# Cache copies moved out of the input projection, and a new order at both ends of the down phase

## The chip, the cores and the metric

One core of one Trainium2 chip runs the whole program. Times are device microseconds of one execution. The five engines are TensorE (PE), VectorE (DVE), ScalarE (ACT), GpSimd (POOL) and SyncE (SP). SP, ACT and POOL start DMA transfers.

## What is computed

One hybrid decoder layer, once on a new prompt of 1024 tokens and once on 8 x 8 new tokens that follow 8192 cached ones. Everything is float32.

```python
def decoder_layer(x, pos, ret_state, k_buf, v_buf, ...):
    z = rmsnorm(x, g_pre_mix) @ w_in                   # 1024 -> 3584
    ... rotary phases on rq, rk; chunkwise retention; group norm; silu gate -> ro
    ... softmax attention, windows (128, 1), (512, 4), (2048, 16), shared bias -> ao
    k_new, v_new = k_all[:, T:], v_all[:, T:]          # the cache, moved on by 8 rows
    x = x + rmsnorm(concat([ro, ao]) @ w_out, g_post_mix)
    gate, up = split(rmsnorm(x, g_pre_ffn) @ w_gu)     # 1024 -> 2 x 2816
    f = (silu(gate) * up) @ w_down                     # 2816 -> 1024
    return x + rmsnorm(f, g_post_ffn), S_new, k_new, v_new
```

The sample's two cache outputs are the inputs moved on by 8 rows: 2040 of 2048 rows of each of 8 sequences are a plain copy from HBM to HBM, 67 MB in all.

## The kernel before

Six stages follow one another: input projection, retention, prompt attention, sample attention, output projection, and the feed-forward part, which has a gate and up phase and a down phase. Each float32 operand is split into a high and a low part (ACT makes the high one, DVE the low one), and PE multiplies high by high, high by low and low by high.

**The cache copies.** `copy_windows` (L127) issues two transfers on POOL's queue, one for the keys and one for the values, of 34 rows of each of 8 sequences: one of 60 shares. Nothing waits for them until the end of the program. Before, 24 shares are issued in the input projection (one after every second tile of z, L343), 32 in the gate and up phase (`PACED`, one or two after the second block of each half group) and 4 in the down phase, after steps 5, 16, 27 and 38.

**Input projection.** For seven groups of 512 columns and nine tiles of rows PE makes z in a PSUM bank, ACT or POOL puts it into one of four buffers `z_out`, and SP stores it to z_scratch. A buffer is free again when its store has landed. Weights of 1 MB per half come on SP's queue.

**Prompt attention.** It has 32 units (four pairs of heads by eight tiles of rows); a pair's later tiles have more keys. For each unit POOL makes two scaled identities `diag` from the softmax denominators, which PE uses two units later. SP loads q, k and v of a pair (512 KB each, in pieces of 512 bytes) while the pair before it runs, and the keys of the second sequence for sample attention after the second pair's. Sample attention loads 5.2 MB of keys and values for each sequence.

**Output projection.** For each tile of rows t, POOL does rstd, the residual sum xm, rstd again and `low` of tile t - 1.

**Gate and up.** Group 0 is apart; groups 1 to 10 (`LAST`) have two half groups of eight blocks, each block a product in the manner of Strassen's seven products. ACT and DVE work six blocks ahead of PE (`LEAD`) into a ring of eight slots (`slot_hi`, `slot_lo`). The last operations of a group give f in six parts, counted by `f_ready`; they read the banks chain_a, chain_b, rest_ps[0] and rest_ps[1]. f and its sums and the differences of w_down go to HBM (`store_f`, `store_f_sums`, `store_t`), since the down phase begins only when all of f is made.

**Down phase.** Seven products P1, P2, P6, P7, P5, P4, P3 of eleven groups each. The first six make 66 steps; a step is four pairs of 128 rows, each three matmuls of 512 columns. Step s needs two operands of 256 KB from HBM, which SP loads into `raw_step[s % 4]` once DVE has made the lows of step s - 4. The bank of pair i in P1 is (x_ps[0], x_ps[1], rest_ps[0], chain_a)[i]; P2 takes chain_b, rest_ps[1] and the two banks of the sample. PE waits in `pair_free` at the first step of each product. The last product P3 has its own 22 blocks, loaded by `load_last(g)` into two buffers `raw_last`, split by `split_last(m)` and `low_last(m)` between the steps' blocks, and used by PE after step 65. `load_last(g)` waits for `low_last(2g - 3)`. SP, like every engine, works through its queue in order.

## Time and profile before

| | us |
|---|---|
| median of 3 runs | 1629.06 |
| lowest and highest | 1626.73 and 1633.83 |
| profiled execution | 1639.63 |
| its span, first to last instruction | 1637.8 |
| PE busy in the span | 1508.8 |
| mean granted clock of PE | 0.972 |

The span is what the trace covers, and its starts are counted from the first instruction. The profiled execution took 10.6 us more than the median. The stages begin at about 0 (input projection), 380 (retention), 463 (prompt attention), 621 (sample attention), 732 (output projection), 850 (gate and up) and 1360 (down). In a timeline row, brackets give the idle time before the instruction and what ended it. The page counts a matmul of 512 columns as 0.39 us, but the next starts 0.23 us after it, as they overlap.

### The profile page before, as it was taken

What the parts mean: (1) busy time and instruction counts of PE and PEld (TensorE: products, weight loads), DVE (VectorE), ACT (ScalarE), POOL (GpSimd) and SP (SyncE); (2) the same over time, 40 slices, a digit from 0 to 9 for tenths busy, and PEclk for the clock granted to TensorE, in tenths of its full rate; (3) what the DMA queues carried; (4) which work ended last, traced back from release to release, by engine and by line L of the source; (5) the groups of instructions that cost most, each with busy time, mean ns of one, the idle gap of its engine ahead of it and who ended that gap; (6) DMA issues with size and microseconds to landing.
All of it is one profiled execution on the core that took longest, in us unless ns stands there. A gap on an engine that the chain in (4) does not pass through costs nothing.

```text
span 1637.8 us, 23157 instructions
## 1 busy us (share of the span) xinstructions
PE 1508.8 (92%) x8974; PEld 1292.8 (79%) x8974; DVE 817.4 (50%) x1380; ACT 555.7 (34%) x1046; POOL 326.3 (20%) x366
## 2 busy tenths in 40 slices
PE   7999999798988888989998899999999997999667
PEld 6788877587845556767888899999999996888546
DVE  2333111103866654543559666666676665554435
ACT  4401112112144443442433333333333432544332
POOL 3265421002532223002554000000000010000001
PEclk9999999899999999999999999999999998999789
DMA  5369899846573108973334679978878787876445
GB/s 204 124 164 234 200 202 216 219 125 220 177 245 120 52 14 332 418 285 107 123 116 161 198 189 177 231 218 237 215 182 240 210 214 232 264 221 201 135 160 180
DMA packets 138253, 317.76 MB, mean 194 GB/s; under 512 B 23884, under 2 KB 65116, under 8 KB 132997
## 3 DMA queue, kind: packets, MB, share of 16 engines
q1 hardware_dynamic: 129352, 229.26, 42.5%
q0 software_dynamic: 6976, 71.32, 21.4%
q10 hardware_dynamic: 1824, 15.83, 2.3%
q8 instruction: 65, 1.06, 0.3%
q14 instruction: 36, 0.29, 0.1%
HBM read 254.45 MB, written 137.92 MB: 240 GB/s over the span
## 4 chain that ended last, share of the span: by engine, by line
PE 36%; DVE 6%; DMA 5%; issue 3%; POOL 3%; ACT 1%; SPq 1%; POOLq 0%; ACTq 0%; DVEq 0%
PE y_ps L2676 25%; PE y_ps L2757 4%; DMA raw_step<-wt_scratch 3%; PE x_ps L2757 2%; DVE slot_lo L2419 2%; DMA raw_step<-w_down 1%; DMA raw<-w_gu 1%; POOL xm L1710 1%; POOL h_lo L1722 1%; PE y_ps L2666 1%; PE y_ps L1841 1%; DVE y L1806 1%; PE m_ps L2757 1%; PE d_ps L2757 1%; PE m_ps L2687 1%
## 5 line engine op out<-in xcount | busy, mean ns | idle before, releaser
L518 PE MATMUL z_ps<-w_hi,h_hi 128*128 128x512 f32 x488 | 191.9, 393 | 17.8 <-ACT z_out L392 11.4
L518 PE MATMUL z_ps<-w_lo,h_hi 128*128 128x512 f32 x488 | 190.9, 391 | 0.0
L2676 PE MATMUL y_ps<-h_hi,slot_hi 128*128 128x320 f32 (+1 forms) x560 | 180.4, 322 | 5.5 <-DVE f L2430 5.5
L2676 PE MATMUL y_ps<-h_hi,slot_lo 128*128 128x320 f32 (+1 forms) x560 | 180.3, 322 | 0.0
L2676 PE MATMUL y_ps<-h_lo,slot_hi 128*128 128x320 f32 (+1 forms) x560 | 180.0, 321 | 0.0
L518 PE MATMUL z_ps<-w_hi,h_lo 128*128 128x512 f32 x432 | 169.0, 391 | 0.0
L131 POOL DMA_DIRECT2D ks_sample<-cache_k_win x60 | 34.0, 567 | 609.9 <-PE y_ps L2676 418.9
L2419 DVE TENSOR_TENSOR slot_lo<-raw_step,slot_hi 128x512 fp32r<-128x512 f32 x132 | 85.4, 687 | 128.0 <-ACT slot_hi L2248 127.9
L518 PEld LDWEIGHTS z_ps<-w_hi,h_hi 128*128 128x128 f32 x488 | 92.3, 189 | 39.4 <-ACT z_out L392 11.9
L2248 ACT CAST slot_hi<-raw_step 128x512 fp32r<-128x512 f32 x132 | 75.4, 619 | 138.1 <-DMA raw_step<-wt_scratch 64.6
L2676 PEld LDWEIGHTS y_ps<-h_hi,slot_hi 128*128 128x128 f32 x560 | 105.7, 189 | 5.7 <-issue 5.7
L2676 PE MATMUL y_ps<-s_hi,slot_hi 128*128 128x384 f32 x320 | 107.6, 336 | 0.0
L2676 PE MATMUL y_ps<-s_hi,slot_lo 128*128 128x384 f32 x320 | 107.6, 336 | 0.0
L2676 PE MATMUL y_ps<-s_lo,slot_hi 128*128 128x384 f32 x320 | 107.5, 336 | 0.0
L518 PEld LDWEIGHTS z_ps<-w_lo,h_hi 128*128 128x128 f32 x488 | 92.2, 189 | 18.9
L2676 PEld LDWEIGHTS y_ps<-h_lo,slot_hi 128*128 128x128 f32 x560 | 105.6, 189 | 0.0
L430 DVE TENSOR_TENSOR w_lo<-w_raw,w_hi 128x2048 fp32r<-128x2048 f32 x14 | 34.2, 2450 | 143.0 <-ACT w_hi L365 143.0
L2676 PEld LDWEIGHTS y_ps<-h_hi,slot_lo 128*128 128x128 f32 x560 | 105.5, 188 | 0.0
L518 PEld LDWEIGHTS z_ps<-w_hi,h_lo 128*128 128x128 f32 x432 | 81.6, 189 | 17.1
L2419 DVE TENSOR_TENSOR slot_lo<-raw,slot_hi 128x512 fp32r<-128x512 f32 x104 | 79.8, 786 | 30.2 <-ACT slot_hi L2248 28.8
L2757 PE MATMUL y_ps<-slot_hi,slot_hi 128*128 128x512 f32 x132 | 55.6, 422 | 15.2 <-DVE f L2454 8.7
L2290 ACT COPY held<-y_ps 128x384 f32<-128x384 f32 x60 | 28.7, 479 | 120.3 <-PE y_ps L2676 120.3
(359 smaller groups left out, 3245.2 us busy)
## 6 DMA issues: line engine op xcount, KB each, us to landing
ks_sample<-cache_k_win POOLq DMA_DIRECT2D x60, 544.0 KB, 9.8
vs_sample<-cache_v_win POOLq DMA_DIRECT2D x60, 544.0 KB, 12.2
raw<-w_gu SPq DMA_DIRECT2D x20, 1024.0 KB, 12.6
raw_step<-f_scratch SPq DMA_DIRECT2D x66, 256.0 KB, 3.8
K<-cache_k_win SPq DMA_DIRECT2D x8, 2048.0 KB
w_raw<-w_in SPq DMA_DIRECT2D x14, 1024.0 KB
z_scratch<-z_out SPq DMA_DIRECT2D x56, 256.0 KB, 5.4
raw_d<-w_down SPq DMA_DIRECT2D x11, 1024.0 KB, 9.3
```

The costliest lines, as they stand in the source:

```text
L131: eng.dma_start(flat(new)[:, bass.ds(row * WID, n * WID)], flat(old)[:, bass.ds(row * WID + DEC_T * WID, n * WID)]).then_inc(kept, 16)
L430: dve.tensor_tensor(w_lo[cut], w_raw[:, q], w_hi[cut].bitcast(F32), ALU.subtract).then_inc(w_lo_ready, 1)
L518: mm = pe.matmul(z_ps[t % 3][:, :], x[:, k, t * 128:t * 128 + 128], w[:, par, k, :], start=(k, n) == first, stop=(k, n) == last)
L1710: pool.tensor_tensor(self.xm[:, t % 2, :], self.y[:, :], self.inputs.x_n[:, t % 2, :], ALU.add).then_inc(self.xm_ready, 1)
L1722: pool.tensor_tensor(self.h.lo[at][cut], self.hg[:, q, :, 0:n], self.h.hi[at][cut].bitcast(F32), ALU.subtract).then_inc(self.lo_ready, 1)
L1806: dve.scalar_tensor_tensor(self.y[0:n, :], src[0:n, :], self.stat[0:n, 2:3], self.g_post[0:n, :], ALU.mult, ALU.mult).then_inc(self.y_read ...
L1841: mm = pe.matmul(self.y_ps[t % 2][:, c:c + 512], x[:, t % 2, k, :], w, start=(k, n) == (0, 0), stop=(k, n) == (KT - 1, len(terms) - 1))
L2248: act.copy(in_slot(slot_hi, n), source(n)).then_inc(hi_ready, 1)
L2290: act.copy(held[:, k, :], chain_a[:, 0:384]).then_inc(held_ready, 1)
L2419: dve.tensor_tensor(in_slot(slot_lo, n), source(n), in_slot(slot_hi, n).bitcast(F32), ALU.subtract).then_inc(lo_ready, 1)
L2676: mm = pe.matmul(bank[:, 0:cols], w, v[:, k, :], start=fresh and (k, m) == (0, 0), stop=(k, m) == (HK - 1, 2), skip_group_check=True)
L2757: mm = pe.matmul(bank, x[:, own], w[:, :], start=fresh and m == 0, stop=ends and m == 2, skip_group_check=True)
```

## The change

The shares of the cache copies are issued elsewhere: none in the input projection, 20 in prompt attention (after `diag` of units 6 to 25), 4 in the output projection (tiles 3 to 6), 30 in the first nine groups of the gate and up phase, and 6 in the down phase (after steps 7, 18, 29, 40, 41 and 52). At the start of the down phase the pairs on rest_ps[0] and chain_a wait for 62 and 64 of `f_ready` in place of 66, and the wait for all 66 stands at P2, which uses the other two banks. SP asks for the operands of step 4 before it stores f and w_down's differences of the last group, and DVE makes the sums of the last f after step 1's blocks. `load_last(g)` comes four steps later in SP's order (after the load of step 48 + 2g), its last two after the loop; `split_last` and `low_last` begin two steps later, with the last two blocks at the end. Handing `kept` through is left out below.

```diff
@@ -132,7 +132,7 @@
                       flat(old)[:, bass.ds(row * WID + DEC_T * WID, n * WID)]).then_inc(kept, 16)
 
 
-SHARE, COPIED_FIRST = (L - DEC_T) // 60, 24
+SHARE = (L - DEC_T) // 60
 
 
 def tile_rows(t):
@@ -336,20 +336,9 @@
                                            ALU.subtract).then_inc(lo_ready, 1)
                     rstd(t)
                 pool.wait_ge(ret.tab_landed, ret.TABS)
-                def copies(k, t):
-
-                    n = at(k, t) - TT
-                    if n % 2 and n < 2 * COPIED_FIRST:
-                        copy_windows(pool, A, kept, n // 2 * SHARE, SHARE)
-
                 for k in (*ROTATED, GATED):
                     for t in range(TT):
                         finish(k, t)
-                        copies(k, t)
-                for k in range(GATED + 1, GROUPS):
-                    for t in range(TT):
-                        pool.wait_ge(z_evac, at(k, t) + 1)
-                        copies(k, t)
 
             @block.scalar
             def _(act):
@@ -1060,6 +1049,8 @@
                     for r in range(2):
                         pool.tensor_scalar(diag[:, g % 2, r], ident[:, :], share[:, g, r:r + 1], None,
                                            ALU.mult).then_inc(diag_ready, 1)
+                    if 6 <= g < 26:
+                        copy_windows(pool, A, kept, (g - 6) * SHARE, SHARE)
 
             @block.scalar
             def _(act):
@@ -1712,6 +1703,8 @@
             pool.tensor_tensor(self.stat[:, 5:6], self.stat[:, 4:5], self.mhalf[:, :], ALU.pow).then_inc(self.xm_rstd, 1)
             if t >= 1:
                 self.low(pool, t - 1)
+            if 3 <= t < 7:
+                copy_windows(pool, self.A, self.kept, (t + 17) * SHARE, SHARE)
 
     def low(self, pool, t):
 
@@ -1969,7 +1962,7 @@
     LAST, RING, LEAD = GROUPS - 1, Count.RING, 6
     LATE_PAIRS = 2
     STEPS = GROUPS * P3
-    PACED = [(24 + 8 * n // 5, 24 + 8 * (n + 1) // 5) for n in range(Count.CHAINS)]
+    PACED = [(24 + 5 * n // 3, 24 + 5 * (n + 1) // 3) for n in range(Count.CHAINS - 2)]
     EARLY_TILES, LATE_TILES = (3, 4, 5, 7), (0, 1, 2, 6)
     FINAL = (PT, 3, 4, 0, 5, 1, 7, 2, 6)
     w_gu = A["w_gu"][0].rearrange("(k p) n -> p k n", p=128)
@@ -2164,12 +2157,14 @@
                     else:
                         load_step(2)
                         load_step(3)
-                    store_t(g)
+                    if g < LAST:
+                        store_t(g)
+                load_step(4)
+                store_t(LAST)
                 store_f(LAST)
-                load_step(4)
                 load_step(5)
+                load_step(6)
                 store_f_sums(LAST)
-                load_step(6)
                 load_step(7)
                 sp.wait_ge(f_stored, 48 * GROUPS)
                 sp.wait_ge(f_sum_ready, 4 * GROUPS)
@@ -2179,8 +2174,10 @@
                 load_x(1)
                 for s in range(8, STEPS):
                     load_step(s)
-                    if s >= GROUPS * P5 and (s - GROUPS * P5) % 2 == 0:
-                        load_last((s - GROUPS * P5) // 2)
+                    if s >= GROUPS * P5 + 4 and s % 2 == 0:
+                        load_last((s - GROUPS * P5 - 4) // 2)
+                load_last(LAST - 1)
+                load_last(LAST)
                 for i, t in enumerate(FINAL):
                     sp.wait_ge(y_ready, i + 1)
                     to = (A["y_prompt"][0, t * 128:t * 128 + 128, :] if t < PT
@@ -2222,15 +2219,15 @@
                                    z[SEQ:NTOK, cols].rearrange("(b t) c -> b t c", b=DEC_B)).then_inc(kept, 16)
                 pool.wait_ge(s3_hi_ready, 1)
                 pool.tensor_tensor(s_lo[2][:, :, :], s_sum[2][:, :, :], s_hi[2][:, :, :].bitcast(F32), ALU.subtract).then_inc(s3_ready, 1)
-                for g in range(1, GROUPS):
+                for g in range(1, LAST):
                     for hh in range(2):
                         pool.wait_ge(done, made(g, hh, 1))
                         copies(*PACED[2 * g - 2 + hh])
                 pool.wait_ge(half_set, 2)
                 root(0)
-                for p in range(4):
-                    pool.wait_ge(done, stepped(GROUPS * p + 5))
-                    copies(56 + p, 57 + p)
+                for p in range(6):
+                    pool.wait_ge(done, stepped(GROUPS * p + 7 if p < 4 else GROUPS * p - 3))
+                    copies(54 + p, 55 + p)
                 for i in range(1, TT):
                     root(i)
                 pool.wait_ge(kept, 16 * (4 + 2 * 60))
@@ -2396,8 +2393,11 @@
                             act.copy(y[PT][0:NS, 512 * c:512 * c + 512], sample_ps[c][NS:128, :]).then_inc(sample_low, 1)
                     split_ahead(Count.step(s) + LEAD)
                     split_ahead(Count.step(s) + 1 + LEAD)
-                    if s >= GROUPS * P5:
-                        split_last(s - GROUPS * P5)
+                    if s >= GROUPS * P5 + 2:
+                        split_last(s - GROUPS * P5 - 2)
+                    if s == STEPS - 1:
+                        split_last(2 * GROUPS - 2)
+                        split_last(2 * GROUPS - 1)
                     if s == 8:
                         square(0)
                     if s == GROUPS * P1 + LAST:
@@ -2613,8 +2613,9 @@
                             times(g, 4, rest_ps[1], 1, 2)
                             add_up(g, 2, 10, 5, 1, 0)
                     sample_low_part(g, 1)
-                sums_of_f(LAST)
                 for s in range(STEPS):
+                    if s == 2:
+                        sums_of_f(LAST)
                     if s == Count.SUMMED_AT:
                         for m in range(4):
                             low_ahead(down(LAST, m) + LEAD)
@@ -2624,8 +2625,11 @@
                             dve.tensor_tensor(y[PT][0:NS, cols], sample_ps[c][0:NS, :], y[PT][0:NS, cols], ALU.add).then_inc(folded, 1)
                     low_ahead(Count.step(s) + LEAD)
                     low_ahead(Count.step(s) + 1 + LEAD)
-                    if s >= GROUPS * P5:
-                        low_last(s - GROUPS * P5)
+                    if s >= GROUPS * P5 + 2:
+                        low_last(s - GROUPS * P5 - 2)
+                    if s == STEPS - 1:
+                        low_last(2 * GROUPS - 2)
+                        low_last(2 * GROUPS - 1)
                     if s == 9:
                         dve.wait_ge(half_set, 2)
                         dve.wait_ge(g_landed, 16)
@@ -2736,9 +2740,10 @@
 
                 def pair_free(p, i):
                     if p == P1:
-                        pe.wait_ge(f_ready, 6 * GROUPS)
+                        pe.wait_ge(f_ready, 6 * LAST + (2 if i == 2 else 4))
                     elif p == P2:
                         pe.wait_ge(c_ready, 3 * Count.CHAINS)
+                        pe.wait_ge(f_ready, 6 * GROUPS)
                         pe.wait_ge(folded, 2)
                     elif p == P6:
                         pe.wait_ge(y_copied, i + 1)
```

## Rows read from the trace of the kernel before

**Rows 1.** The page's first part: busy us (share of the span) and instructions of each engine.
```profile
PE 1508.8 (92%) x8974; PEld 1292.8 (79%) x8974; DVE 817.4 (50%) x1380; ACT 555.7 (34%) x1046; POOL 326.3 (20%) x366
```
**Rows 2.** Waits of PE, whole span: total us, times, longest us.
```profile
PE x_ps L2757 <- DVE slot_lo L2419: 20.2, 6, 4.9
...
PE y_ps L2757 <- DVE f L2454: 8.7, 1, 8.7
```
**Rows 3.** Windows, input projection: from:to, length, each engine's busy us (x), PEclk, DMA, GB/s.
```profile
176.00:210.00 34.00, 34.00 (x151) 28.15 (x150) 2.29 (x1) 5.71 (x7) 8.18 (x10) 1.00 0.97 223
200.00:300.00 100.00, 97.87 (x430) 80.38 (x430) 12.72 (x6) 19.27 (x24) 16.33 (x23) 1.00 0.97 203
315.00:325.00 10.00, 8.16 (x25) 6.53 (x26) 2.29 (x1) 3.71 (x4) 1.10 (x2) 0.65 0.72 248
346.00:354.00 8.00, 8.00 (x37) 6.64 (x36) 0.00 (x0) 0.69 (x1) 1.10 (x2) 1.00 0.65 204
```
**Rows 4.** Timeline of PE at 316; then z_out, the store issued at 280.94.
```profile
316.84 0.79 PE L518 MATMUL z_ps<-w_hi,h_hi 128*128 128x512 f32 x1 [11.44 <-ACT z_out L392]
...
DMA to landing us min/median/max: 35.1/35.1/35.1
```
**Rows 5.** Windows in prompt attention and one in sample attention, columns as in rows 3.
```profile
510.00:530.00 20.00, 16.53 (x122) 10.20 (x124) 13.27 (x37) 11.05 (x27) 5.90 (x10) 1.00 0.71 238
545.00:560.00 15.00, 12.70 (x96) 7.93 (x96) 10.01 (x30) 7.89 (x20) 5.51 (x10) 1.00 0.52 140
...
650.00:700.00 50.00, 46.70 (x674) 36.50 (x673) 25.41 (x41) 24.15 (x49) 0.00 (x0) 1.00 1.01 417
```
**Rows 6.** Timelines of POOL, SP and PE in both attentions: start, us, instruction, idle before.
```profile
495.69 1.18 POOL L1061 TENSOR_SCALAR diag<-ident,share 128x128 f32<-128x128 f32 x2 [4.86 <-PE O_ps L1229]
...
584.97 1.18 POOL L1061 TENSOR_SCALAR diag<-ident,share 128x128 f32<-128x128 f32 x2 [1.66 <-DVE share L1155]
...
509.95 0.43 SPq L965 DMA_DIRECT2D q_n<-z_scratch  x1
...
534.39 1.06 PE L1186 MATMUL T_ps<-ident,q_n 128*128 128x128 f32 x8
...
571.02 1.04 PE L1186 MATMUL T_ps<-ident,q_n 128*128 128x128 f32 x8
...
644.17 3.27 PE L1460 MATMUL T_ps<-ident,K 128*128 128x128 f32 x28 [1.55 <-DMA K<-z_scratch]
```
**Rows 7.** Timelines of POOL, ACT and PE, start of the down phase; a window of it.
```profile
1342.88 0.55 POOL L131 DMA_DIRECT2D ks_sample<-cache_k_win  x1 [21.43 <-PE y_ps L2676]
...
1363.91 0.62 ACT L2248 CAST slot_hi<-raw_step 128x512 fp32r<-128x512 f32 x1 [10.48 <-DMA raw_step<-w_down]
...
1370.55 0.80 PE L2757 MATMUL y_ps<-slot_hi,slot_hi 128*128 128x512 f32 x1 [8.69 <-DVE f L2454]
...
1370.00:1380.00 10.00, 9.45 (x29) 7.51 (x30) 6.92 (x12) 3.03 (x6) 0.00 (x0) 0.66 0.86 293
```
**Rows 8.** Down phase: a window, then timelines of PE and ACT.
```profile
1400.00:1480.00 80.00, 79.80 (x350) 65.13 (x349) 42.22 (x66) 36.92 (x67) 3.88 (x7) 1.00 0.75 235
...
1481.57 0.39 PE L2757 MATMUL x_ps<-slot_hi,slot_hi 128*128 128x512 f32 x1
...
1597.79 0.63 PE L2757 MATMUL y_ps<-last_hi,last_hi 128*128 128x512 f32 x1
...
1463.21 0.62 ACT L2248 CAST slot_hi<-raw_step 128x512 fp32r<-128x512 f32 x1 [2.69 <-DMA raw_step<-wt_scratch]
...
1516.85 0.62 ACT L2248 CAST slot_hi<-raw_step 128x512 fp32r<-128x512 f32 x1 [7.16 <-DMA raw_step<-wt_scratch]
```
**Rows 9.** The tile m_n, its two loads issued from 756.3 to 757.
```profile
DMA to landing us min/median/max: 5.2/5.3/5.4
```
**Rows 10.** The page's last part: DMA issues, size of each, median us to landing.
```profile
raw<-w_gu SPq DMA_DIRECT2D x20, 1024.0 KB, 12.6
```

More of the change, by code:

```diff
@@ L977, in __call__, with prompt_attention @@
         return self.nc.alloc_sbuf_tensor_at(name, shape, dtype, offset=here)
-def prompt_attention(nc, A, z, mix_t, bias, ident, q_n, k_n, qk_landed, clear, ahead, second_keys, spare, retained, state_s, S_out, sout_ready):
+def prompt_attention(nc, A, z, mix_t, kept, bias, ident, q_n, k_n, qk_landed, clear, ahead, second_keys, spare, retained, state_s, S_out, sout_ready):
     UNITS, LAST = NPAIR * PT, NPAIR * PT - 1
@@ L1633, with __init__ @@
 class OutProjection:
-    def __init__(self, nc, ctx, A, x_mid, h, ident, inputs, w_b):
+    def __init__(self, nc, ctx, A, x_mid, h, ident, kept, inputs, w_b):
         at = lambda n, s, o, d=F32: nc.alloc_sbuf_tensor_at(n, s, d, offset=o)
@@ L1638, in __init__ @@
         sem = lambda n: nc.alloc_semaphore("p5_" + n)
-        self.A, self.x_mid, self.h, self.ident, self.inputs, self.w_b = A, x_mid, h, ident, inputs, w_b
+        self.A, self.x_mid, self.h, self.ident, self.kept, self.inputs, self.w_b = A, x_mid, h, ident, kept, inputs, w_b
         self.m_hi = at("m_hi", [128, 2, KT, 128], Layout.M_SPLIT, F32R)
@@ L1981, in out_and_ffn @@
         ps = lambda n, s: ctx.enter_context(nc.psum_tensor(n, s, F32))
-        out = OutProjection(nc, ctx, A, x_mid, h, ident, inputs, w_b)
+        out = OutProjection(nc, ctx, A, x_mid, h, ident, kept, inputs, w_b)
         sem = lambda n: nc.alloc_semaphore("p6_" + n)
@@ L2857, in load_first_window @@
             sp.dma_start(q_s[:, :], z[SEQ:NTOK, 4 * WID:5 * WID]).then_inc(q_landed, 16)
-        prompt_attention(nc, A, z, mix_t, bias_p, ident, q_n, k_n, qk_landed, clear_padding, load_first_window,
+        prompt_attention(nc, A, z, mix_t, kept, bias_p, ident, q_n, k_n, qk_landed, clear_padding, load_first_window,
                          lambda sp: load_keys(sp, A, z, K, K_landed, 1),
```

## The prediction

> **What bounds the kernel now.** I read the page first, then PE's waits, then windows of the four stretches that the edits touch. PE is busy 92% of the span [rows 1], so only time in which PE stands or runs at the low clock can be won. The longest waits of PE are six in the down phase for slot_lo and one for f at its start [rows 2], and one of 11.4 us late in the input projection [rows 4]. All three lead to DMA. Matmuls of 512 columns come every 0.228 us at full clock (430 in 97.87 us, rows 3; 350 in 79.8 us, rows 8). The profiled execution took 1639.63 us, 10.6 us over the median of 1629.06; I sum against its trace and take the difference from the median.
>
> **Prices.** A cache share is two transfers of 544 KB, 1.11 MB. One alone fills the window 346 to 354 at a DMA share of 0.65 [rows 3], so it takes 5.2 us of all 16 DMA engines; I use 5.4 (queue start included), 205 GB/s. Beside SP's transfers both are slower. In the window 176 to 210 all engines together moved 223 GB/s at a share of 0.97 [rows 3]; three shares are 98 of it, which leaves SP's queue 125, part of it moved while no copy was pending. SP's loads alone run at about 320 GB/s (0.75 of the engines carry 235 in the down phase, rows 8). I use 100 GB/s for SP's queue while copies are pending.
>
> **1. Input projection: 24 shares go.** ACT waited for a free z_out because a store landed 35.1 us after its issue; PE stood 11.44 us [rows 4]. Then the granted clock was low: 25 matmuls took 8.16 us between 315 and 325 [rows 3], 2.5 us over 0.228 each. From 200 to 300 PE stood 2.1 us more. Sum 16.0 us. Without copies SP's queue there has 2 MB of weights, 1 MB of zr and nine stores of 256 KB in 49 us, under 120 GB/s: nothing is late next. Gain 16, bounds 11 and 16.
>
> **2. Prompt attention: 20 shares come, one after each of the units 6 to 25.** In the trace these units' diag operations run from 495.69 to 584.97 [rows 6]: 89 us for 20 x 5.4 = 108 us of DMA. POOL's own 1.1 us for the two issues lies in its idle time before the next diag (1.1 us at the shortest), so PE pays nothing for it; if POOL's queue filled, POOL would hold back diag and PE, but then the copies are done earlier, and the balance below stays.
> The other traffic here is 0.71 x 20 + 0.52 x 15 [rows 5] and some 2 us of stores, 24 us. Together 132 us from 497, to 629. While both run, the window 176 to 210 does 98/205 + 125/320 = 0.87 of the work that the engines could; the 24 us last some 63 us then and lose 8. So the queue is empty at 637. Sample attention begins at 621.3 and runs at 417 GB/s with a DMA share of 1.01 [rows 5], and its keys landed 1.55 us late already [rows 6]: what is left over delays it one for one, 16 us.
> Inside the stage: the q and k rows of the third pair are asked for at 509.95 and used at 534.39, those of the fourth at 546 and used at 571.02 [rows 6]. At 100 GB/s the first 1.57 MB land at 528, in time; the values and second keys hold the queue until 557, and the fourth pair's rows land at 574: 3.5 us late, and some slow clock. I take 5. **Cost 21 us.** Below, if the engines take the copies in beside the rest without loss and finish at 629: 9 us. Above: 50 us, if SP's queue gets 60 GB/s: the third pair's rows come 2 us late and the fourth's 43.
>
> **3. Output projection: 4 shares.** POOL has 2.9 us free after low in each tile. The rows of the next tile landed after 5.2 to 5.4 us [rows 9] and were used at once, so they have no slack; but they are asked for some 8 us after low, when the copy (7 us) is through. Cost 1 us, bounds 0 and 8.
>
> **4. Gate and up.** 30 shares over 18 half groups in place of 32 over 20: the same two or one per half group, and PE never stood there. Nothing.
>
> **5. The start of the down phase.** Two shares were issued from 1342.88, and a load of w_down for step 2, issued at 1343.31, held ACT for 10.48 us until 1363.91; DVE's last f came behind it, and PE, which wants all six f before its third pair, stood 8.69 us [rows 7]. Then 29 matmuls took 9.45 us at a granted clock of 0.66, 2.8 us over 0.228 each [rows 7]. The change removes both: the last group has no copies, and the third and fourth pairs wait for the second and fourth f only, which free their banks. Next late would be the lows of steps 0 to 2 or the loads of steps 5 and 7, asked for behind stores of f and of its sums; load 4 goes out 20 us earlier, and sums_of_f (four operations of 0.7 us) moves to step 2, where DVE has two steps in hand. Gain 11.5, bounds 7 and 12.
>
> **6. The last product's blocks.** PE begins step 39 at 1481.57 and the last product at 1597.79 [rows 8]: 116.2 us for 27 steps of 12 x 0.228 = 2.74, 74.0 us. So 42 us are lost. The reason is in SP's order. load_last(g) at s = 44 + 2g waits for low_last(2g - 3), which DVE does at its step 41 + 2g; the load of step 45 + 2g queues behind it and is wanted at DVE's next step. So every two steps hold one full trip from issue to landing, and ACT stands 7.16 us in it [rows 8]. After the change the wait at s = 48 + 2g ends at DVE's step 43 + 2g, and the load of step 49 + 2g is wanted at 46 + 2g: two steps lie between. A trip of 6 us, 0.63 us of ACT and 2.5 of DVE make 9 us for three steps, and with one step of DVE (1.9 us) 11 for four; PE needs 10.9. So PE may just set the pace. But the traffic is then 1.57 MB in two steps, 288 GB/s, and two shares (57 and 58) are issued at steps 40 and 41 and one at 52. One share alone made ACT wait 2.69 us for a load and cost PE 0.6 [rows 8]: it ate the 6 us in hand. Two hold SP's queue to 100 GB/s for 16 to 20 us, while 4.9 MB are wanted: 9 us; the one at 52 costs 4; slow clock 2 to 3. Residue 16 of 42. **Gain 26 us**, bounds 14 (every trip lengthened) and 38.
> The last product's blocks 9 and 10 come after the loop; its first pass needs block 10 only after 10 x 3 x 0.228 = 6.8 us, which covers that load. The tail of 1637.8 - 1597.8 = 40 us stays.
>
> **Sum.** -16 + 21 + 1 - 11.5 - 26 = -31.5 us, or 1598 us.
>
> **The rivals.**
> (a) The copies fit: prompt and sample attention pay 5 us, and the down phase 5. For it: the engines are idle half of 495 to 621. Against: 89 us for 108. -16 + 5 - 11.5 - 37 = -59.5, 1570 us.
> (b) The down phase stays bound by loads: a trip of 9 us (a share's neighbours took 8 to 9.7) makes 13.4 us for four steps, 3.35 each, over 18 steps 11 us more. 1609 us.
> (c) The wait at the start stays, on something else late in DVE's chain; PE then waits some 9 us as now. 1609 us.
> (d) Slower. The DMA engines take turns between the copies' queue and SP's by pieces, not by bytes. In 176 to 210 SP's queue moved about 1660 pieces of 2 KB in 34 us, 49 per us. q and k of one pair are 2048 pieces of 512 bytes: 42 us, landing at 552 where 534 is wanted, 18 us late. For the fourth pair the values (21 us), keys and store (11) and q and k (42) come to 626 against 589, 37 late. With the clock 61 us in place of 21, and nothing left for the next stage: 1638 us. It decides once SP's queue moves fewer than some 85 pieces per us beside copies. Against it: the gate and up loads of 1 MB are 1024 pieces of 1 KB, most of them issued within 1 us of one or two shares, and landed after 12.6 us in the median [rows 10]: some 97 per us, twice the pieces at the same bytes.
> The Trainium skill says, in "DMA: Bandwidth & Descriptors", section "Queues, rings and completion order", that each engine goes round the queues by packets of about 9 to 17 descriptors, whatever they hold. By that rule (d) would hold, as 512 byte rows make the smallest packets; the trace of before has no such rows beside copies, so it neither agrees nor disagrees. The same page, "Issuing engines are not separate DMA queues", says transfers from all engines share 16 DMA engines, which rows 3 and 5 bear out.
>
> **How the numbers follow.** Forecast 0.50 (1598, own range 1582 to 1612), (a) 0.14, (b) 0.15, (c) 0.05, (d) 0.11, something not seen 0.05. The range 1572 to 1626 leaves out (d) and most of (a)'s lower half. A measurement of this kernel tells about 0.5%, 8 us, from no change. Faster by more than that: the forecast, (a), (c) and nearly all of (b), 0.81. Within it 0.09, slower 0.10.
>
> **What would show it.** Right: no wait of PE for z_out; PE going on at the third pair of step 0 without a pause; ACT's waits for raw_step under 3 us from step 48 on but for two places behind the shares; the start of sample attention near 625 less 16, with keys 10 us or more late in its first periods. The prediction is wrong if prompt attention has long waits for q_n and k_n (d), if none of its transfers is late (a), or if raw_step still holds ACT in every pair of steps (b).

## The result, and the profile after

The changed kernel takes 1667.47 us in the median of four runs (1664.31 to 1676.02), the kernel before 1627.89 in the median of four beside them. The ratio is 1.026, 95% interval 1.019 to 1.034: slower by about 40 us, where 1598 us and faster was forecast. The profiled execution took 1664.31 us.

The page's first part and its DMA queues (part 3: packets, MB, share of 16 engines) of the changed kernel:

```profile
PE 1492.7 (90%) x8974; PEld 1284.4 (77%) x8974; DVE 816.2 (49%) x1380; ACT 556.6 (33%) x1046; POOL 327.1 (20%) x366
...
q1 hardware_dynamic: 129352, 229.26, 41.0%
q0 software_dynamic: 6976, 71.32, 23.4%
```

PE works 16 us less than in [rows 1] in a span that is 25 us longer. q1 is SP's queue; q0 is POOL's, nearly all of it the copies. Waits of PE in the changed kernel:

```profile
PE T_ps L1177 <- DMA k_n<-z_scratch: 82.9, 2, 42.7
...
PE x_ps L2762 <- DVE slot_lo L2419: 4.6, 2, 4.3
...
PE z_ps L507 <- POOL h_lo L335: 4.3, 3, 1.8
...
PE y_ps L2762 <- DVE slot_lo L2419: 1.0, 1, 1.0
```

The waits of [rows 2] have become small: 4.6 us for slot_lo on the banks x_ps in place of 20.2, and f at the start of the down phase is gone. The wait for z_out of [rows 4] is gone too. In their place stand two waits for k_n, 82.9 us, half of the time in which PE isn't busy (1662.5 - 1492.7 = 169.8). Timelines of the changed kernel show them (PE and SP; in brackets the idle time before):

```profile
442.65 1.09 PE L1177 MATMUL T_ps<-ident,q_n 128*128 128x128 f32 x8 [1.07 <-POOL ones L1043]
...
487.50 0.43 SPq L954 DMA_DIRECT2D q_n<-z_scratch  x1
487.98 6.14 SPq L954 DMA_DIRECT2D k_n<-z_scratch  x1
494.16 51.45 SPq L1018 DMA_DIRECT2D v_n<-z_scratch  x1
...
552.15 1.97 PE L1177 MATMUL T_ps<-ident,q_n 128*128 128x128 f32 x8 [40.19 <-DMA k_n<-z_scratch]
...
567.71 1.06 SPq L954 DMA_DIRECT2D k_n<-z_scratch  x1
...
635.19 1.97 PE L1177 MATMUL T_ps<-ident,q_n 128*128 128x128 f32 x8 [42.67 <-DMA k_n<-z_scratch]
...
687.74 4.99 PE L1451 MATMUL T_ps<-ident,K 128*128 128x128 f32 x44 [0.34 <-PEq L1009]
```

Rows asked for at 487.5 come at 552, and SP stands for 51 us in the very next issue. Prompt attention begins 21 us earlier than before (442.65 against 463.59) and ends 66 us later (687.74 against 621.29): it takes 245.1 us in place of 157.7.

Lengths of the stretches, each from the first matmul of a stage to that of the next (step 39 by counting 468 matmuls; the last stretch to the end of the span):

| | before | after |
|---|---|---|
| start to prompt attention | 463.6 | 442.7 |
| prompt attention | 157.7 | 245.1 |
| sample attention to gate and up | 739.0 | 740.5 |
| down phase, to step 39 | 121.3 | 108.9 |
| step 39 to the last product | 116.2 | 82.2 |
| last product to the end | 40.0 | 43.1 |

-20.9 + 87.4 + 1.5 - 12.3 - 34.0 + 3.1 is the 24.8 us between the two spans. Every part but one won what it should or more; the last stretch, which was to stay, grew by 3.1 us.

### The profile page after: what moved, and what is told of

The parts are those of the page before. It is cut to its first block, busy times and chain, and to the rows that moved or that the text cites. A ratio compares the mean times of both kernels' runs of the same rounds, so it can differ in the third digit from the quotient of the medians.

```text
span 1662.5 us, 23144 instructions
## 1 busy us (share of the span) xinstructions
PE 1492.7 (90%) x8974; PEld 1284.4 (77%) x8974; DVE 816.2 (49%) x1380; ACT 556.6 (33%) x1046; POOL 327.1 (20%) x366
## 4 chain that ended last, share of the span: by engine, by line
PE 36%; DVE 5%; POOL 3%; DMA 3%; issue 3%; ACT 1%; SPq 1%; POOLq 0%; ACTq 0%; DVEq 0%
PE y_ps L2680 26%; PE y_ps L2762 4%; PE x_ps L2762 3%; DMA raw_step<-wt_scratch 2%; DVE slot_lo L2419 2%; POOL xm L1701 1%; DMA raw<-w_gu 1%; POOL h_lo L1715 1%; PE y_ps L2670 1%; PE y_ps L1834 1%; DVE y L1799 1%; PE m_ps L2691 1%; PE d_ps L2691 1%; DVE y L2519 1%; SPq L2108 0%
## 5 line engine op out<-in xcount | busy, mean ns | idle before, releaser
L419 DVE TENSOR_TENSOR w_lo<-w_raw,w_hi 128x2048 fp32r<-128x2048 f32 x14 | 32.0, 2289 | 124.1 <-ACT w_hi L354 124.1
L1177 PE MATMUL T_ps<-ident,q_n 128*128 128x128 f32 x32 | 6.2, 355 | 83.9 <-DMA k_n<-z_scratch 82.9
L1050 POOL TENSOR_SCALAR diag<-ident,share 128x128 f32<-128x128 f32 x64 | 37.9, 599 | 175.0 <-DVE share L1146 133.8
## 6 DMA issues: line engine op xcount, KB each, us to landing
raw_d<-w_down SPq DMA_DIRECT2D x11, 1024.0 KB, 12.3
```

The source lines that it names most:

```text
L419: dve.tensor_tensor(w_lo[cut], w_raw[:, q], w_hi[cut].bitcast(F32), ALU.subtract).then_inc(w_lo_ready, 1)
L1050: pool.tensor_scalar(diag[:, g % 2, r], ident[:, :], share[:, g, r:r + 1], None, ALU.mult).then_inc(diag_ready, 1)
```

## What holds the rows back: the trace of the changed kernel

The windows of the first wait (columns as in rows 3):

```profile
487.50:530.00 42.50, 20.90 (x158) 13.21 (x158) 17.02 (x44) 12.89 (x30) 13.96 (x25) 0.85 1.02 159
530.00:552.00 22.00, 0.00 (x0) 0.00 (x0) 0.00 (x0) 0.00 (x0) 0.00 (x0) 0.50 0.89 154
```

The DMA engines are full, but at 159 GB/s. The packets tell whose they are. DMA queues of the changed kernel from 500 to 515, and then from 545 to 554 (packets, MB, share):

```profile
DMA packets 344, 1.89 MB, mean 126 GB/s; under 512 B 125, under 2 KB 289, under 8 KB 291
...
q0 software_dynamic: 171, 1.78, 94.5%
q1 hardware_dynamic: 171, 0.09, 3.8%
...
q1 hardware_dynamic: 2607, 2.28, 83.0%
q0 software_dynamic: 43, 0.10, 5.5%
```

In the first window one packet of SP's queue (some 520 bytes) goes for one packet of the copies (10.4 KB on the mean): 171 and 171, and 199 and 199 between 580 and 600. SP gets 6 GB/s. The mean of 10.4 KB mixes two sizes: only 53 of the 344 packets hold 8 KB or more, and 51 of them, of 34 KB each, carry the copies' 1.78 MB; their other 120 are under 512 bytes. In the second window the copies are through, and SP's queue moves 2607 packets in 9 us. The landings agree: the share issued at 511.4 landed at 546.6 (keys) and 549.9 (values), q at 549.3 and k at 552.1; in the second case the last values landed at 633.7, q at 632.8 and k at 635.1. **The rows land when the pile of copies is through.**

The trace of the kernel before had shown the same in small. A load of w_gu in pieces of 1 KB was issued at 935.1, with two shares behind it. Its DMA queues from 935 to 940, and then from 940 to 948:

```profile
q1 hardware_dynamic: 1005, 1.02, 62.8%
q0 software_dynamic: 40, 0.56, 38.3%
...
q0 software_dynamic: 95, 1.11, 99.5%
q1 hardware_dynamic: 35, 0.03, 3.1%
```

Nearly the whole load had gone by 940, when the copies' packets filled the engines; the last few dozen packets took until 948.3.

The second cause is the pile itself. The first two shares, issued 6 us apart, landed after 5.9 to 7.0 us. From the fourth on (issued every 3 to 6 us) each landed 8.6 us after the one before, on the mean: nine issued between 474 and 511 were through at 550, where 5.4 us each would have made 523. From the rows of 500 to 515, a 34 KB packet held its engine for an estimated 4.4 us (94.5% of 16 x 15 us, by 51).

## The experiments

### The parts one by one

Theory 1: the copies in prompt attention do it, by turns of packets. Its rivals: the amount of bytes, or the order in SP's own queue. The first four runs have 1631.09 us (seven runs) as their time before.

```diff
-                    if 6 <= g < 26:
-                        copy_windows(pool, A, kept, (g - 6) * SHARE, SHARE)
```

> The changed kernel without the 20 shares of prompt attention; they are left out, so 20 of 60 shares of the two cache outputs are not written. Every theory that puts the loss on these copies expects both waits of PE for q_n and k_n (40.2 and 42.7 us) gone and the low clock beside them too: sample attention starts 82.9 + some 4 us earlier, and the whole takes about 1664 - 87 = 1577 us. If the q and k rows are late for another reason (the order in SP's queue, a wait before their issue), one of the two waits stays and the time is above 1610 us.

Measured: 1582.66 us, ratio 0.970 (0.964 to 0.975). No wait for k_n; q and k land after 4.8 and 6.1 us, and the stage takes 159.4 us. The order in SP's queue is that of the changed kernel, so it is not the cause.

```diff
-                    if 6 <= g < 26:
-                        copy_windows(pool, A, kept, (g - 6) * SHARE, SHARE)
...
-            if 3 <= t < 7:
-                copy_windows(pool, self.A, self.kept, (t + 17) * SHARE, SHARE)
...
+                    if n % 2 and n < 2 * COPIED_FIRST:
+                        copy_windows(pool, A, kept, n // 2 * SHARE, SHARE)
```

> The changed kernel with its 24 shares of prompt attention and output projection back in the input projection, as in the kernel before. Parts 2 and 3 are undone, and so is part 1. What is left is the new start of the down phase and the later asking for the last product's blocks, which the trace of the changed kernel puts at some 42 us from sample attention to the end: about 1628 - 40 = 1588 us. If the down phase's gain came from the shares' new places in gate and up and down alone it would be the same here; if it came from PE having been slow or late earlier in the changed kernel, 1610 us or more.

Measured: 1594.14 us, ratio 0.977 (0.971 to 0.983), 37 us below its own runs of before and 6 above the number given. The wait for z_out is back (12.0 us). From sample attention to the end it takes 976.6 us, the changed kernel 974.8, the kernel before 1016.5: the gain of the down phase has nothing to do with the early shares. Against e1_no_att_copies, which has none there, the 24 shares in the input projection cost 11.5 us.

The kernel before with its 24 early shares in their new places:

```diff
-SHARE, COPIED_FIRST = (L - DEC_T) // 60, 24
+SHARE = (L - DEC_T) // 60
...
+                    if 6 <= g < 26:
+                        copy_windows(pool, A, kept, (g - 6) * SHARE, SHARE)
...
+            if 3 <= t < 7:
+                copy_windows(pool, self.A, self.kept, (t + 17) * SHARE, SHARE)
```

> The kernel before with only its first 24 shares moved: none in the input projection, 20 in prompt attention, 4 in the output projection; gate, up and down are as before. Parts 1, 2 and 3 alone. From the two traces: the input projection wins 21 us, prompt attention loses 87, the output projection about nothing: 1628 + 66 = 1694 us. If the losses in the changed kernel had come from elsewhere, about 1634 us, as predicted for these three parts.

Measured: 1705.64 us, ratio 1.046 (1.040 to 1.051), 12 us above the number given; prompt attention began at 448.9 here, 6 us later than in the changed kernel, and the rest wasn't looked into. Waits for k_n of 81.5 us, the stage 244.0 us, and the waits for slot_lo of before are still there. Together with e1 and e2 this puts the loss on these 20 shares alone.

### Turns by packets

```diff
+def copy_rows(eng, A, kept, row, n):
+    rows = lambda name, at: A[name][0].rearrange("b l h d -> l b (h d)")[at:at + n]
+    for new, old in (("ks_sample", "cache_k_win"), ("vs_sample", "cache_v_win")):
+        eng.dma_start(rows(new, row), rows(old, row + DEC_T)).then_inc(kept, 16)
...
-                        copy_windows(pool, A, kept, (g - 6) * SHARE, SHARE)
+                        copy_rows(pool, A, kept, (g - 6) * SHARE, SHARE)
```

> The changed kernel with the 20 shares of prompt attention asked for in pieces of 2 KB (row by row) in place of pieces of some 10 KB; the bytes are the same. Theory 1, the engines take turns between the queues by pieces: a turn of the copies then carries a fifth of the bytes, SP's 512-byte pieces go some two to five times as fast while both are pending, and the two waits of PE for k_n fall from 83 us together to under 35; about 1610 us, and sample attention finds some copies left over. Theory 2, the engines share by bytes or the sum of all transfers sets the time: the waits stay within 5 us of 83, or grow if small pieces make the copies dearer: 1660 us or more. POOL may take longer to issue a copy; if that holds diag back, PE's waits for diag say so.

Measured: 1693.61 us, ratio 1.038 (1.032 to 1.044). Its longest wait of PE, and its DMA queues from 505 to 518, when copies were pending throughout:

```profile
PE O_ps L1222 <- POOL diag L1057: 97.8, 6, 24.5
```
```profile
DMA packets 4358, 2.56 MB, mean 197 GB/s; under 512 B 2198, under 2 KB 3984, under 8 KB 4350
...
q0 software_dynamic: 2534, 1.52, 56.0%
q1 hardware_dynamic: 1824, 1.05, 32.3%
```

The packets of the copies are now of 600 bytes on the mean. Again two sizes are mixed: 366 packets of 4 KB carry nearly all of the 1.52 MB (twice the 2 KB I had asked for, about an eighth of 34 KB), and the rest are under 512 bytes. SP's queue gets 1.05 MB in 13 us, 81 GB/s in place of 6. Fewer shares were pending here than in the changed kernel's window (under two, where it had four or five), but the copies moved as fast, 117 GB/s against 119. q and k of the third pair land after 16.2 and 24.5 us in place of 61.8 and 64.1, and no wait for k_n is left. So the turn theory holds: the same bytes in small packets let SP through. The time missed theory 1's 1610 by 84 us, by another way of starving: POOL stood for up to 23 us in issuing a copy, and diag behind it. That its queue took no more is the likely reason, not shown. The shares landed 10.9 us apart on the mean.

### The down phase

Both are e2_copies_back with one part undone; the runs before them took 1634.5 us in the median. The first excerpt leaves out that the later loads among the stores, the sums of f and `PACED` (now 30 shares over 20 half groups) go back too.

```diff
-                for g in range(1, LAST):
+                for g in range(1, GROUPS):
...
-                load_step(4)
-                store_t(LAST)
+                store_t(LAST)
                 store_f(LAST)
+                load_step(4)
...
-                        pe.wait_ge(f_ready, 6 * LAST + (2 if i == 2 else 4))
+                        pe.wait_ge(f_ready, 6 * GROUPS)
```

> The kernel of e2_copies_back (both new ends of the down phase, copies of the attention back in the input projection), with the old start of the down phase: copies in the last group too (30 over 20 half groups), the loads of steps 4 to 6 behind the stores, all six f before PE's third pair, the sums of the last f before step 0. The difference to e2_copies_back prices part 5. If the prediction's 11.5 us are right: 1594 + 11.5 = 1605.5 us, with a wait of PE for f near 9 us at the start. If the wait at the start moves elsewhere (rival c): 1596 us. If the start is worth more than predicted, 1609 us or more.

Measured: 1596.27 us, ratio 0.974 (0.970 to 0.978): 2 us from e2_copies_back, less than these runs tell apart, so the old order alone is not worth the 11.5 us. The wait for f is 2.3 us. To step 39 it takes 113.1 us, where e2_copies_back takes 108.9 and the kernel before 121.3. The two differ from before in the copies too: one share in the last group's first half in place of two. That needn't be what made the 8 us: e3_copies_only has the old start with the very copies of before, and takes 115.9 us, with waits of 4.7 us for f and 6.5 us of ACT for the load of [rows 7] (before 8.7 and 10.5, here 2.3 and 4.1). So the old start costs 4 to 12 us over the new one, by the kernel that it stands in, and what part the copies have in it isn't shown.

```diff
-                    if s >= GROUPS * P5 + 4 and s % 2 == 0:
-                        load_last((s - GROUPS * P5 - 4) // 2)
-                load_last(LAST - 1)
-                load_last(LAST)
+                    if s >= GROUPS * P5 and (s - GROUPS * P5) % 2 == 0:
+                        load_last((s - GROUPS * P5) // 2)
...
-                    if s >= GROUPS * P5 + 2:
-                        low_last(s - GROUPS * P5 - 2)
+                    if s >= GROUPS * P5:
+                        low_last(s - GROUPS * P5)
```

> The kernel of e2_copies_back with the last product's blocks asked for as before (load_last two steps after each other from step 44 on, split and made low two steps earlier); shares stay where e2_copies_back has them. The difference prices part 6. From sample attention to the end the changed kernel won some 40.5 us by parts 5 and 6; if the start took 11.5 of them, this one is 29 us slower than e2_copies_back: 1623 us, with six waits of PE for slot_lo of some 20 us together as before. By the predicted 26 us it would be 1620, by the bound of 14 it would be 1608.

Measured: 1635.08 us, ratio 1.000 (0.998 to 1.002): by the two ratios some 38 us slower than e2_copies_back, more than the 29 I had left for this part. Waits of PE, and the last product's first matmuls:

```profile
PE x_ps L2761 <- DVE slot_lo L2421: 19.6, 6, 4.6
...
PE y_ps L2761 <- DVE slot_lo L2421: 11.9, 4, 4.4
```
```profile
L2761 PE MATMUL y_ps<-last_hi,last_hi x22: 387/389/398, 1597.4 to 1611.9; 128*128 128x512 f32 x22
```

From step 39 to the last product the old order takes 124.1 us here, the new one 83.9. In the kernel before it took 116.2, and in e3_copies_only 117.6. The shares of steps 40, 41 and 52 stand in this stretch only in the changed kernel and those made from it; they are what differs, and the old order takes 6.5 to 8 us more with them.

### The same 20 shares elsewhere

From the landings so far I took a share for 6 us, and the pile for SP's transfers only. Both kernels are the changed one with other units:

```diff
-                    if 6 <= g < 26:
-                        copy_windows(pool, A, kept, (g - 6) * SHARE, SHARE)
+                    if g in PLACES:
+                        copy_windows(pool, A, kept, PLACES.index(g) * SHARE, SHARE)
```

> The changed kernel with the same 20 shares in prompt attention after other units: 5 to 7, 12 to 15, 19 to 31 in place of 6 to 25, so that no more than one is pending when SP asks for the q and k rows of a pair, and the last pair, in which SP loads nothing, takes eight. Theory 1 (turns by pieces, so that 512-byte rows starve whenever copies stand beside them): both waits for k_n go, the stage costs no more than the 3 to 8 us by which the last copies reach into sample attention: 1583 + 6 = 1589 us, with both bounds 1583 and 1600. Theory 2 (108 us of copies are too much for this stage wherever they stand): the stage keeps more than half of its loss, 1625 us or more.

> As e7_20_elsewhere, with 16 shares in prompt attention (units 5, 6, 13 to 15, 19 to 22, 24 to 30) and four in the input projection (after tiles 5, 17, 29 and 41 of z). Theory 1: nothing of the 16 is late, sample attention starts on time, and four shares 66 us apart hold no store of z for longer than some 10 us, so the input projection pays nothing: 1583 us, within 4. If even single shares cost the input projection time (the 24 cost 11.5 us, about 0.5 each), 1585 us. If theory 2 holds, 1610 us or more.

Measured: 1649.03 us (ratio 1.007, 1.004 to 1.009) and 1622.67 us (0.992, 0.989 to 0.994). Both miss theory 1 as I had priced it, by 60 and 40 us, and lie where theory 2 put them. Waits of PE in e7_20_elsewhere, a timeline of POOL at the start of sample attention, and three windows with little but copies in them:

```profile
PE T_ps L1451 <- PEq L1009: 41.6, 1, 41.6
PE T_ps L1177 <- DMA k_n<-z_scratch: 25.8, 1, 25.8
```
```profile
671.98 0.52 POOL L1336 MEMSET V_second<- 128x512 f32 x1 [48.84 <-POOLq L1009]
```
```profile
478.00:484.00 6.00, 4.97 (x41) 4.03 (x39) 4.53 (x12) 3.70 (x9) 2.16 (x5) 1.00 0.56 192
603.00:625.00 22.00, 17.86 (x148) 12.22 (x145) 13.00 (x29) 9.53 (x19) 9.68 (x18) 1.00 1.02 123
...
633.00:670.00 37.00, 0.00 (x0) 0.00 (x0) 0.00 (x0) 0.00 (x0) 0.00 (x0) 0.51 0.91 121
```

Three things are read here. First, from 603 to 625 SP moves next to nothing (6 packets), and the copies still run at 122 GB/s, 9.1 us per share: the shares issued between 592.7 and 622.0 land 8.7 to 10.8 us one after the other, while those issued at 472.6, 478.6 and 484.8 land 6.2 us after one another (keys). The pile is dear without SP: at the early shares (478 to 484) 192 GB/s move with the engines 56% busy, in the pile 123 with all of them busy. Second, the fourth pair's rows, q asked for at 527.8 while two shares were pending and k at 536.7, with four more shares from 537 on, landed after 31 and 42 us. Third, after PE's last matmul at 630 nothing runs on any engine until 672.0; the last share landed at 670.0. In e8_16_att_4_in the last landed at 641.7 and the next stage began at 643.3. **This stage did not end before the copies that POOL issued in it had landed.** That was in no theory of mine, and against what the description of the kernel says, that nothing waits for them until the end of the program.

With this the number of shares counts too. From the first issue to the last landing the 20 shares took 197 us (472.6 to 670.0) and the 16 of e8_16_att_4_in 167 (474.8 to 641.7), 10 us each. By estimate from these, a stage that asks for its first share at 474 and ends by itself at some 605 has room for 13.

### The pile, tested

The pile theory now: alone a share lands in 7 us, in a pile it costs 9.1; in a pile SP gets one packet for one. The rival is the amount: a share costs 8.8 us wherever it stands. The runs before took 1632.33 us (eleven).

```diff
-                    if 6 <= g < 26:
-                        copy_windows(pool, A, kept, (g - 6) * SHARE, SHARE)
+                    if g in (5, 6, 7, 13, 14, 15, 20, 21, 22, 23, 25, 27, 29):
+                        copy_windows(pool, A, kept, (7 + PLACES.index(g)) * SHARE, SHARE)
...
+                    if n % 7 == 3 and n < 49:
+                        copy_windows(pool, A, kept, n // 7 * SHARE, SHARE)
```

> The changed kernel with its 24 early shares as 13 in prompt attention (after units 5 to 7, 13 to 15, 20 to 23, 25, 27, 29), 7 in the input projection (after every seventh tile of z from tile 3 on) and 4 in the output projection. What the traces so far show: a share that is alone lands in 7 us and the next follows every 6.1 us, but in a pile each takes 9.1; and in a pile SP's queue moves one packet for one packet of the copies (171 and 171 in 500 to 515 of the changed kernel). Here shares of the attention stand at least 5.5 us apart, none is pending when SP asks for q and k, and the last lands some 10 us before the stage ends. Pile theory: no wait for k_n, none for the store of O_T, input projection nearly free: 1583 us, within 6. If what counts is the amount in the stage (13 x 9.1 = 118 us beside 24 of other loads in 155 us) there are late loads again and it is 1600 us or more.

Measured: 1584.29 us, ratio 0.970 (0.966 to 0.974). The stage takes 156.3 us, no more than with no share in it; q and k land after 6 to 9 us. The shares of the last two groups of units did pile up (8 to 10 us each from 555 on), but the last landed at 603.3, before SP's last store of O_T (604.7), and sample attention began at 605.1. This run has fewer shares (13, for which the estimate above finds room) and other places at once, so it shows that 13 can be had for nothing, and not which of the two did it.

```diff
                     if 6 <= g < 26:
+                        pool.wait_ge(kept, 32 * (g - 6))
                         copy_windows(pool, A, kept, (g - 6) * SHARE, SHARE)
```

> The changed kernel, where POOL waits before each of its 20 shares in prompt attention until the one before has landed, so that there is never a pile. POOL's wait holds back diag, and so PE. Pile theory: a share takes some 7 us from issue to landing, 20 of them 140 us where units 6 to 25 take 89; PE stands for diag, 50 us in all, and SP's rows get through in the gaps between two shares: the waits for k_n are under 15 us together, and the time is 1630 to 1645 us. Amount theory (a share costs 8.8 us wherever it stands): 176 us, a stage as long as in the changed kernel or longer, 1665 us or more.

Measured: 1654.44 us, ratio 1.012 (1.006 to 1.017). Its longest wait of PE, and the landing of k_n asked for at 567.2:

```profile
PE O_ps L1216 <- POOL diag L1050: 54.9, 10, 14.7
```
```profile
DMA to landing us min/median/max: 9.9/9.9/9.9
```

No wait for k_n is left, as the pile theory says, and PE waits for diag, 54.9 us. With one pending at a time keys land after 5.5 to 6.2 us (twice, beside SP's loads, 10), and values, issued 0.6 us behind them, mostly 7 to 9 us after their own issue: a share makes 8.7 us in all, not the 7 I had taken. So the time lies 9 us above the range that I gave the pile theory and 11 below the amount theory's, and tells the two less well apart than the waits do: the copies take nearly as long as in the pile, but SP's rows land in the gaps, after 7 to 10 us in place of 62 to 67.

```diff
-                    if 6 <= g < 26:
+                    if 6 <= g < 26 and g % 2 == 0:
                         copy_windows(pool, A, kept, (g - 6) * SHARE, SHARE)
```

> The changed kernel with only every second of its 20 shares in prompt attention (after units 6, 8, ... 24); the other ten are left out, so ten of 60 shares of the two cache outputs are not written. If the loss goes with the number of shares (87 us for 20), 43 us stay: 1625 us. Pile theory: shares are 8.9 us apart on the mean, most land before the next is issued, the q and k rows get through between them in less than the 24 us in hand: no wait of PE for k_n over 3 us, and 1583 us, within 8.

Measured: 1588.0 us, ratio 0.974 (0.969 to 0.979). Half the shares cost 6 us more of stage (165.4 us against 159.4 with none), not 43: the loss is not in proportion to the number. Ten stay under the 13 for which the stage has room, so this fits both the pile theory and that count. The one wait for k_n is 6.5 us, more than the 3 I gave; those rows landed after 21 and 30 us behind shares 5 us apart.

### The rest of the down phase

```diff
-                    pool.wait_ge(done, stepped(GROUPS * p + 7 if p < 4 else GROUPS * p - 3))
+                    pool.wait_ge(done, stepped(6 * p + 7))
```

> The kernel of e9_13_paced with the six shares of the down phase after steps 7, 13, 19, 25, 31 and 37, so none in the stretch in which the last product's blocks are loaded, and no two beside each other. From step 39 to the last product e9_13_paced takes 84.9 us where 27 steps alone take 74.0, with waits of PE for slot_lo of 4.7 and 0.8 us in it. If the shares at steps 40, 41 and 52 make that residue, as the prediction's part 6 had it, the stretch falls to under 78 us and the time to 1584 - 7 = 1577 us. If the residue comes from SP's own loads (1.57 MB in two steps), it stays at 82 or more, and the time is the same as that of e9_13_paced, 1584 us.

Measured: 1570.71 us, ratio 0.963 (0.959 to 0.966), beside 1631.08 for the kernel before; 6 us below the number given. From step 39 (1456.2) to the last product it takes 74.1 us, as many as the matmuls alone:

```profile
L2773 PE MATMUL y_ps<-last_hi,last_hi x22: 387/389/398, 1530.3 to 1544.8; 128*128 128x512 f32 x22
```

No wait for slot_lo is left there, and the last stretch takes 40.7 us in place of 43.2. The residue goes with the three shares. This kernel has all 60 shares; it is 60 us faster than the one before, and some 100 faster than the changed one.

## Why the prediction was wrong

**Part 1**, 16 us (11 to 16): right. Prompt attention begins at 459.1 to 464.7 in the four kernels with 24 shares in the input projection (before, e2, e5, e6; mean 461.7) and at 442.7 to 449.1 in the seven with none (after, e1, e3, e4, e7, e10, e11; mean 446.8): 15 us. The 21 us between the two profiled runs of before and after is at the upper edge of that.

**Part 2**, 21 us (9 to 50): 87.4, and the step that failed. Two terms of it were mis-sized, and one inference was wrong.
- *The price of a share.* 5.4 us came from one share that stood alone [rows 3], with 0.52 MB of SP's in the same window: of its DMA share of 0.65 the copies had 0.47. So alone a share takes even less than I had, but in a pile 8.6 to 9.3 us. 20 of them are some 175 us in a window of 89, where I had 108. The landings of before had hinted at it: between 219 and 307 nine shares, issued 9.7 us apart beside 92 GB/s of SP's, landed 10.9 us apart, most of them 13 to 17 us after their issue.
- *SP's queue beside copies.* 100 GB/s was taken from a stretch (176 to 210) with one or two shares pending, whose packets held the engines for 49% of the time, and SP moved pieces of 2 KB in between. In a pile, at 94.5%, it is 6 GB/s at 512-byte pieces. The inference "at 100 GB/s the rows land at 528" should have been: they land when the pile is through, 9 shares after 474, at 550.
- That what is left over delays sample attention one for one was never tested by the changed kernel, since PE's stops let the copies catch up; e7_20_elsewhere shows it, by the end of the stage and not by late keys. That the balance stays the same when POOL is held in issuing doesn't fit e4_copies_2k, where PE stood 97.8 us for diag.

**Part 3**, 1 us, and **part 4**, nothing: right; sample attention to the start of the down phase takes 1.5 us more. PE did stand in gate and up, where I had said that it never does: 3.9 us for slot_lo and 5.5 for f in the kernel before, 3.9 and 4.5 in the changed one.

**Part 5**, 11.5 us (7 to 12): 12.3 between the two profiles. That it came so close is partly luck: over the new start's 108.9 us the old one takes 12.3 more in the kernel before, 7.0 in e3_copies_only and 4.2 in e5_old_start.

**Part 6**, 26 us of 42 (14 to 38): 34.0. The mechanism was right, a load waiting behind load_last in every second step, and so was the cause of the residue; its size was not. 16 us were forecast, 8.2 stayed, and e12_down_even takes them away. The tail of 40 us did not quite stay: 43.1. It is 40.7 in e12_down_even (new order, no late shares) and 39.7 in e6_old_last (old order, late shares), so it takes both. In these two and in the changed kernel PE is through with the stretch's matmuls after 30.4 us, so the 3 us lie behind PE; where, was not looked into.

**The rivals.** (a), (b) and (c) fell. (d) named the place and the kind of thing: q and k rows starve beside copies, stalls in the third and fourth pair, 1638 us. It had a chance of 0.11, 61 us where 87 came, and its working was wrong: 49 pieces per us, taken from [rows 3] (where the trace has 1945 packets in 34 us, 57 per us), were 11.4 (171 in 15 us), because a turn lasts as long as a packet of the copies, and those that carry data are of 34 KB. By that rate 2048 pieces would take 180 us; the end of the pile saved them. What I held against (d) was [rows 10]: 97 pieces per us beside one or two shares. The row is a median over loads with and without shares beside them, and where shares were, as at 935, 1005 packets had gone by 940 and the last few dozen took 8 us more. So the row was no evidence against (d). By the Trainium skill ("DMA: Bandwidth & Descriptors", section "Queues, rings and completion order") an engine goes round the queues packet by packet and drains a whole packet before it switches. The equal counts of 171 and 171, and of 199 and 199, agree with that, though the 0.72 of SP's packets per packet of the copies in e4_copies_2k show that the counts need not be equal when packets are small.

## What to carry to other kernels

Before transfers are moved into a stretch that looks half idle, work out when the pile that they form there will be through, at the price of a transfer inside a pile, and treat any small-row load issued meanwhile as landing at that time. Count first how many the stretch can hold at that price, and let the last one land before the stage ends. Then place them: here in short runs of shares 6 us apart, none pending when the rows on the path are asked for. Both counted. The same 20 shares made the stage 86 us longer than with none in one set of places and 66 in another (e7_20_elsewhere); 16 in places much like the second's made it 35 longer, and 13 cost nothing.

## What the runs showed of the hardware

- Copies of 1.11 MB from HBM to HBM, three of them issued 6 us apart, followed each other every 6 to 7 us (192 GB/s at a DMA share of 0.56); in a pile they took 8.6 to 9.3 us each on the mean, with or without other traffic (e7_20_elsewhere, 603 to 670: 121 to 123 GB/s at shares of 1.02 and 0.91). By estimate from the shares and the packets, a 34 KB packet held its engine for 1.6 us in the first case (56.0% of 16 x 6 us by 33) and 4.6 in the second (101.3% of 16 x 22 us by 77). Why is open.
- SP's queue and POOL's moved 171 packets each in 15 us. Those of SP had some 520 bytes; of POOL's 51 had 34 KB and 120 were under 512 bytes. With data packets of 4 KB in the copies SP's queue got 81 GB/s in place of 6. The store of O_T, 512 KB in rows of 4 KB, which lands in 2.6 us in the kernel before, took 30.0 us beside a pile.
- With the shares asked for row by row (e4_copies_2k) POOL stood 17 to 23 us in issuing, five times, with two to three shares pending; with packets of 34 KB it issued a share with five pending (e7, at 622) and didn't stand.
- The next stage began 1.6 to 2.0 us after the last copy of the stage had landed, on every engine, in the two kernels in which a copy landed last (e7, e8); PE stood 41.6 and 38.3 us for it. In the other twelve, copies or none, sample attention began 0.45 to 0.52 us after SP's last store of O_T had landed.
